# A two-block transformer kernel on one core: the shift of the modulation as products, squares on VectorE, work moved at three seams

## What is computed

```python
mod = (jnp.dot(jax.nn.silu(c), w_ada[l]) + b_ada[l])[:, None, :]
sh1, sc1, g1, sh2, sc2, g2 = jnp.split(mod, 6, axis=-1)
h = rmsnorm(x, norm_mix[l]) * (1.0 + sc1) + sh1
proj = jnp.dot(h, w_in[l])
...
x = x + g1 * jnp.dot(merged, w_out[l])
h2 = rmsnorm(x, norm_ffn[l]) * (1.0 + sc2) + sh2
y = hierarchical_moe(h2, ...)        # 4 groups x 8 experts, top 2 of a group
x = x + g2 * y
x = rmsnorm(x, norm_final)
...
h = rms_norm(x, norm1_g[l])          # second block: window attention and pooling
x = x + jnp.concatenate([a, b], axis=-1) @ w_out[l]
h2 = rms_norm(x, norm2_g[l])
x = x + peer(h2, ...)                # 16384 small experts, 8 heads x 16 of them per token
```

## Time and profile before

| | us |
|---|---|
| median of 3 runs | 2891.45 |
| lowest and highest | 2890.89, 2893.74 |
| the profiled execution's own time | 2890.11 |
| its span | 2888.3 |
| TensorE busy in it | 2725.0 (94%) |
| VectorE busy | 2064.0 (71%) |
| ScalarE busy | 1385.0 (48%) |
| GpSimd busy | 958.6 (33%) |

### The profile page before, as it was taken

One profiled execution on the slowest core, in us unless ns is written; L12 is line 12 of the kernel. 1 busy time (PEld: TensorE's weight loads), 2 busy tenths in 40 slices (PEclk: granted clock), 3 DMA queues, 4 the chain that ended last, 5 costly groups with the idle time before them and its releaser, 6 DMA issues. The chain is left out here.

```text
span 2888.3 us, 35914 instructions
## 1 busy us (share of the span) xinstructions
PE 2725.0 (94%) x13955; PEld 2395.2 (83%) x13955; DVE 2064.0 (71%) x2764; ACT 1385.0 (48%) x1865; POOL 958.6 (33%) x498
## 2 busy tenths in 40 slices
PE   5999998895999999999798899999999999999999
PEld 3778875684788888874676689999999999999999
DVE  7366645535898899970663589998888778888884
ACT  3232124422777777761342334368888633333332
POOL 2425441232222222220211347723333334444430
PEclk8999999996999999999889999999999999999999
DMA  6336321113899999975310325579999999999993
GB/s 264 102 122 243 117 88 44 54 51 140 315 370 382 389 373 359 361 299 242 137 44 1 117 85 171 183 266 343 347 349 353 358 350 372 380 364 375 371 351 110
DMA packets 173277, 703.45 MB, mean 244 GB/s; under 512 B 24720, under 2 KB 52016, under 8 KB 138800
## 3 DMA queue, kind: packets, MB, share of 16 engines
q1 hardware_dynamic: 89856, 459.49, 43.5%
q0 software_dynamic: 47232, 142.66, 13.3%
q10 hardware_dynamic: 36016, 98.97, 9.2%
HBM read 657.50 MB, written 72.88 MB: 253 GB/s over the span
## 5 line engine op out<-in xcount | busy, mean ns | idle before, releaser
L134 PE MATMUL psum<-h_high,pe_high 128*128 128x384 f32 (+1 forms) x1664 | 570.1, 343 | 15.3 <-DVE h_low L2412 9.4
L135 PE MATMUL psum<-h_low,pe_high 128*128 128x384 f32 (+1 forms) x1664 | 564.6, 339 | 0.0
L136 PE MATMUL psum<-h_high,pe_low 128*128 128x384 f32 (+1 forms) x1664 | 564.5, 339 | 0.0
L2148 ACT ACTIVATE pe_high<-ring 128x1024 fp32r<-128x1024 f32 x272 | 287.2, 1056 | 324.0 <-PE psum L136 323.6
L2275 DVE TENSOR_TENSOR pe_low<-ring,pe_high 128x1024 fp32r<-128x1024 f32 x216 | 264.5, 1225 | 191.3 <-ACT pe_high L2148 185.3
L128 POOL TENSOR_TENSOR mx_slab_low<-mx_half_slab,mx_slab_high 128x1024 fp32r<-128x1024 f32 x88 | 223.6, 2543 | 409.6 <-ACT mx_slab_high L119 395.5
L134 PEld LDWEIGHTS psum<-h_high,pe_high 128*128 128x128 f32 x1664 | 313.7, 188 | 21.5 <-issue 10.2
L1343 DVE TENSOR_TENSOR slab_low_moe<-half_slab_moe,slab_high_moe 128x2048 fp32r<-128x2048 f32 x126 | 285.6, 2289 | 50.2 <-ACT slab_high_moe L1292 50.1
L136 PEld LDWEIGHTS psum<-h_high,pe_low 128*128 128x128 f32 x1664 | 313.4, 188 | 5.2
L135 PEld LDWEIGHTS psum<-h_low,pe_high 128*128 128x128 f32 x1664 | 313.5, 188 | 4.6
L2033 POOL DMA_INDIRECT pe_rows<-in_v_rows,pe_place x128 | 204.0, 1594 | 258.5 <-DVE pe_sums L2382 222.0
(11 more groups left out here) (452 smaller groups left out, 5949.1 us busy)
## 6 DMA issues: line engine op xcount, KB each, us to landing
half_slab_moe<-in_weights SPq DMA_DIRECT2D x128, 1024.0 KB, 9.3
ring<-in_weights SPq DMA_DIRECT2D x162, 512.0 KB, 4.6
hT<-in_weights SPq DMA_DIRECT2D x64, 1024.0 KB, 7.4
ring<-in_v_rows SPq DMA_DIRECT2D x128, 512.0 KB
mx_half_slab<-in_weights SPq DMA_DIRECT2D x44, 1024.0 KB, 5.1
gates_rows<-pe_table ACTq DMA_DIRECT2D x12, 2048.0 KB, 10.5
pe_gt<-gates_rows ACTq DMA_DIRECT2D x16, 1536.0 KB
gelu_rows<-pe_gl ACTq DMA_DIRECT2D x30, 768.0 KB
```

Of the source, the lines that this page charges most:

```text
L134: pe.matmul(out, w[0], x[0], start=start, stop=False)
L135: pe.matmul(out, w[0], x[1], start=False, stop=False)
L136: return pe.matmul(out, w[1], x[0], start=False, stop=stop)
L2148: act.activation(high[:, g % RING, :], raw[:, g % RING, :], ACT.Copy).then_inc(highs, 1)
```

## The change

Four parts.

1. **Opening.** The shift half of the modulation becomes 16 fp32 products on TensorE: silu(c) spread over 128 columns (`c_wide`, 8 chunks) by the shift's weights (`w_shift`, 4 loads of 1 MB), two halves of 512; the wanted columns are taken out with the identity and a reduction on VectorE. They stand between the sums of squares and the distance products. The 8 scale columns remain dots; the root's reciprocal now stands ahead of them. The transfer of `c` as a row stands behind that of the constants.
2. **Mixer output.** The squares and their sum over chunks are made on VectorE behind each residual; four one-column products at the end give the sums per token.
3. **Route.** The wide root goes: the per-token root is spread over a diagonal (`spread_of`) and multiplied by ones, one fp32 product. The first slab's low part is on VectorE, in two halves (`first_low`), one ahead of the table's reading and one behind the names. Turns use two pairs of banks.
4. **Seams.** The waits for the experts' last landings go from the end of the experts to the end of overflow. The `share` matrices are made on VectorE at the start of overflow. The squares at the head of peer are made on VectorE in attend's output loop, with one product at that stage's end; ScalarE's root stands first in peer.

```diff
+            def scale_column(n):
+                if n >= 4:
+                    sp.wait_ge(dotted, n - 3)
+                c = 8 + n
+                sp.dma_start(ada[n % 4], d.w_ada[c // 4][:, (c % 4) * D:(c % 4 + 1) * D]).then_inc(ada_in[n % 4], 16)
...
+            for i in range(4):
+                sp.dma_start(w_shift[:, 2 * i:2 * i + 2, :], d.w_shift[:, 2 * i:2 * i + 2, :]).then_inc(w_shift_in[i], 16)
+            for n in range(4):
+                scale_column(n)
+            slab_half(0, 0)
+            for n in range(4, 8):
+                scale_column(n)
+            slab_half(0, 1)
...
+            pe.wait_ge(c_widened, 1)
+            for k in range(DC):
+                if k % 2 == 0:
+                    pe.wait_ge(w_shift_in[k // 2], 16)
+                for i in range(2):
+                    mm = pe.matmul(m.bank[i][:, :], c_wide[:, k, :], w_shift[:, k, i * 512:(i + 1) * 512],
+                                   start=(k == 0), stop=(k == DC - 1))
+            mm.then_inc(shift_mm, 1)
...
-                              start=(k == 0 and t == 0), stop=False)
-                pe.wait_ge(x_squared, k + 1)
-                for t in range(TT):
-                    pe.matmul(m.bank[4][:, 36 * TT + t:36 * TT + t + 1], x_squares[:, k % 2, t * P:(t + 1) * P], m.ones[:, 0:1],
-                              start=False, stop=(k == DC - 1 and t == TT - 1))
-                pe.matmul(m.bank[5][:, :], m.ones, x_squares[:, k % 2, :], start=(k == 0), stop=(k == DC - 1)
-                          ).then_inc(x_used, 1)
+                              start=(k == 0 and t == 0), stop=(k == DC - 1 and t == TT - 1))
...
+            pe.wait_ge(x_squared, 1)
+            for t in range(TT):
+                pe.matmul(m.bank[4][:, 36 * TT + t:36 * TT + t + 1], x_squares[:, 0, t * P:(t + 1) * P], m.ones[:, 0:1],
+                          start=True, stop=True)
...
+            act.dma_start(c_cols[:, :], d.c_cols).then_inc(cols_in, 16)
+            act.dma_start(m.const[:, :], d.const).then_inc(const_in, 16)
             act.dma_start(c_row, d.c.to_broadcast([P, D])).then_inc(c_in, 16)
...
+            act.wait_ge(cols_in, 16)
+            act.activation(c_wide, bcast(c_cols[:, :], 2, P), ACT.Silu).then_inc(c_widened, 1)
             act.wait_ge(x_in, 16)
             for k in range(DC):
                 act.activation(work[:, k, :], m.xT[:, k, :], ACT.Square).then_inc(squares_sem, 1)
+            act.wait_ge(c_in, 16)
+            act.activation(c_act, c_row, ACT.Silu).then_inc(c_ready, 1)
...
-            for i in range(8):
-                if i < 4:
-                    act_high(m, act, S_OUT + 1, i, 0)
-                act.wait_ge(mix_done, 9 + i)
-                if i >= 2:
-                    act.wait_ge(x_used, i - 1)
-                act.activation(x_squares[:, i % 2, :], m.xT[:, i, :], ACT.Square).then_inc(x_squared, 1)
+            for j in range(4):
+                act_high(m, act, S_OUT + 1, j, 0)
...
-            dve.wait_ge(c_ready, 1)
-            for t in range(6):
-                dots(t)
             dve.wait_ge(root, 1)
             chain(dve.reciprocal(rstd, rstd))
-            dots(6)
-            dots(7)
+            dve.wait_ge(c_ready, 1)
+            for n in range(4):
+                dot(n)
...
+            dve.wait_ge(shift_mm, 1)
+            own_columns = junk.rearrange("p (f n) -> p f n", n=P)
+            chain(dve.tensor_tensor(own_columns, m.psum[:, 0:2, :].rearrange("p b (f n) -> p (b f) n", n=P),
+                                    bcast(m.ident, 1, DC), ALU.mult))
+            chain(dve.tensor_reduce(m.raw[:, 0:8], own_columns, AX.X, ALU.add))
+            for n in range(4, 8):
+                dot(n)
...
+                chain(dve.scalar_tensor_tensor(out=m.xT[:, i, :], in0=m.bank[i % 4][:, :], scalar=m.mod[:, 16 + i:17 + i],
+                                               in1=m.xT[:, i, :], op0=ALU.mult, op1=ALU.add))
+                dve.sem_inc(mix_done, 1)
+                chain(dve.tensor_tensor(x_squares[:, min(i, 1), :], m.xT[:, i, :], m.xT[:, i, :], ALU.mult))
+                if i >= 1:
+                    chain(dve.tensor_tensor(x_squares[:, 0, :], x_squares[:, 0, :], x_squares[:, 1, :], ALU.add))
+            dve.sem_inc(x_squared, 1)
...
-            half = SLAB // 2
-            for h in range(2):
-                pool.wait_ge(m.highs, 4 * S_MOE + 2 * h + 2)
-                pool.tensor_tensor(m.low[:, 0, h * half:(h + 1) * half], m.half_slab[:, h, :],
-                                   m.high[:, 0, h * half:(h + 1) * half].bitcast(F32), ALU.subtract).then_inc(m.lows, 2)
...
-                if t >= 1:
-                    pe.wait_ge(rows_ready, 2 * t)
+                if t >= 2:
+                    pe.wait_ge(rows_ready, 2 * (t - 1))
                 for k in range(DC):
-                    mm = pe.transpose(m.bank[5 + k // 4][:, (k % 4) * P:(k % 4 + 1) * P], hT[:, k, t * P:(t + 1) * P],
+                    mm = pe.transpose(m.bank[2 * (t % 2) + k // 4][:, (k % 4) * P:(k % 4 + 1) * P], hT[:, k, t * P:(t + 1) * P],
...
+            pe.wait_ge(spread_ready, 1)
+            pe.matmul(m.bank[5][:, :], m.ones, flat(spread_of), start=True, stop=True).then_inc(spread, 1)
...
-            act.activation(rstd[:, :], m.bank[5][:, :], ACT.Sqrt, bias=m.eps[:, :], scale=1.0 / D).then_inc(root, 1)
...
+            def first_low(h):
+                dve.wait_ge(m.highs, 4 * S_MOE + 2 * h + 2)
+                dve.tensor_tensor(m.low[:, 0, h * half:(h + 1) * half], m.half_slab[:, h, :],
+                                  m.high[:, 0, h * half:(h + 1) * half].bitcast(F32), ALU.subtract).then_inc(m.lows, 2)
...
+            dve.tensor_tensor(spread_of[:, :, :], bcast(m.ident, 1, TT), bcast(col_std[:, :], 2, P), ALU.mult).then_inc(spread_ready, 1)
...
-            dve.wait_ge(root, 2)
-            chain(dve.reciprocal(rstd[:, :], rstd[:, :]))
+            dve.wait_ge(spread, 1)
             for k in range(DC):
                 dve.scalar_tensor_tensor(out=hT[:, k, :], in0=xT[:, k, :], scalar=scale[:, k:k + 1],
-                                         in1=rstd[:, :], op0=ALU.mult, op1=ALU.mult).then_inc(scaled, 1)
+                                         in1=m.bank[5][:, :], op0=ALU.mult, op1=ALU.mult).then_inc(scaled, 1)
...
+            first_low(0)
...
+            first_low(1)
...
-                pool.wait_ge(m.over_x_in[i], 16)
-                pool.wait_ge(y_out[i], 16 * E // 2)
...
-            pe.wait_ge(shares, 1)
...
+            pe.matmul(m.bank[5][:, :], m.ones, sq[:, 0, :], start=True, stop=True)
...
-                    last = dve.tensor_scalar(share[:, i, t, :], m.ident, m.pair_w[:, i, t:t + 1], None, ALU.mult)
-            last.then_inc(shares, 1)
...
+                chain(dve.tensor_tensor(m.xT[:, j, :], m.bank[j][:, :], m.xT[:, j, :], ALU.add))
+                chain(dve.tensor_tensor(sq[:, min(j, 1), :], m.xT[:, j, :], m.xT[:, j, :], ALU.mult))
+                if j >= 1:
+                    chain(dve.tensor_tensor(sq[:, 0, :], sq[:, 0, :], sq[:, 1, :], ALU.add))
+            dve.sem_inc(x_squared, 1)
...
-                pe.wait_ge(squares, norm * DC + k + 1)
-                mm = pe.matmul(m.bank[5][:, :], m.ones, work[:, k, :], start=(k == 0), stop=(k == DC - 1))
-            mm.then_inc(total, 1)
...
-                act.activation(work[:, k, :], xT[:, k, :], ACT.Square).then_inc(squares, 1)
+            act.activation(rstd[:, :], m.bank[5][:, :], ACT.Sqrt, bias=m.eps[:, :], scale=1.0 / D).then_inc(root, 1)
             split(0)
             split(1)
-            act.wait_ge(total, norm + 1)
-            act.activation(rstd[:, :], m.bank[5][:, :], ACT.Sqrt, bias=m.eps[:, :], scale=1.0 / D).then_inc(root, 1)
             split(2)
             split(3)
...
+            sp.wait_ge(m.over_gu[0], 32)
...
+                pool.wait_ge(m.over_x_in[i], 16)
+                pool.wait_ge(m.moe_y_out[i], 16 * EXPERTS // 2)
...
+            share = m.run[:, :, :].rearrange("p a (t n) -> p a t n", n=P)
+            for i in range(2):
+                dve.tensor_tensor(share[:, i, :, :], bcast(m.ident, 1, TT), bcast(m.pair_w[:, i, :], 2, P), ALU.mult)
```

75 lines of the change are left out of this document (32 added, 43 removed).

## The result

| | before | changed |
|---|---|---|
| median, us | 2891.43 | 2865.31 |
| lowest to highest (4 runs each) | 2890.89 to 2893.74 | 2863.64 to 2866.79 |
| span of the profiled execution | 2888.3 | 2865.0 |

The ratio is 0.9911, with an interval of 0.9899 to 0.9923: 26.1 us less, 0.9%. The prediction was 2867.9, with 2857 to 2877.

The account below looks back on a forecast made before the run. Long TensorE-bound stages with seams where TensorE waits for chains on other engines and landings; +4.0 - 12.7 - 12.4 - 3.0 - 0.9 + 1.5 = -23.5, from 2890.11 to 2866.6, plus 1.3 for the median: 2867.9, range 2857 to 2877.

Parts of the forecast that it names:

- Opening: Kernel start to first feature product: shift products on TensorE delay it, +4.0 us, ends -1.4 and +6.
- Mixer output: Mixer's output stage: shorter steps -10.6 us and a shorter tail -2.1, together -12.7, ends -14.7 and -10.8.
- Route: Route stage, starting at R (668.3 before): gather at R+29.7 instead of R+42.1, -12.4 us, ends -14 and -7.
- four of them 7.1, and the same 4.5: Route: four turns at pitch 1.77, then 4.5 us for table and names, would allow the gather at R+27.6.
- (a): Experts to overflow: GpSimd's waits for landings moved a stage later, -3.0 us, ends -3.3 and -1.5.
- (b): Overflow to attend: shares made earlier, the second row load's landing then latest, -0.9 us, range -1.5 to 0.
- (c): Attend to peer, whose stage starts at B: new head costs +1.5 us, ends -1.9 and +2.9.
- The tie: Peer head, starts 0.03 us apart: VectorE first, product at B+15.1 (+0.4); GpSimd first, B+17.6 (+2.9).
- VectorE first: Rival at the peer head: VectorE goes before GpSimd, net +0.4 instead of +1.5, total 2866.8; chance 0.12.
- the rule named beside it: Trainium skill, peer head: first issuer holds the shared pair all instruction, the other fully blocks; VectorE ahead gives +0.4.
- the opening was not hidden: Rival that opening costs 0 instead of +4.0 and route gets -14: -29.1, 2862.3 us; chance 0.18.
- no long stage ran at half clock: Slower-clock rival: experts' or peer's work at granted clock 0.50 cancels the gain or gives 2897; chance 0.04.

Follow-up runs that it names:

- run 4: The changed kernel with VectorE doing all 8 dots of the scale before it waits for the shift's products; 2863.6 us.
- Run 9: The kernel before with only the mixer output's squares and sum on VectorE, plus one more wide ones-product at its end; one execution 2880.9 us.
- run 2: The changed kernel with the peer head as before (8 squares on ScalarE, 8 products behind the barrier); 2863.4 us.
- run 3: The changed kernel with the peer head's wide root kept in PSUM, so a scaling has one SBUF input; 2861.2 us, 0.9893 of before.
- run 5: The changed kernel with the first expert slab's low part back on GpSimd, in front of the gather; one execution 2874.0 us.
- run 6: The changed kernel with the route's four turns on one pair of banks as before; one execution 2867.1 us.
- run 7: The changed kernel with GpSimd's waits for the last landings back at the experts' end, and that stage's own y tile; one execution 2868.2 us.
- run 8: The changed kernel with the 8 share instructions back at the start of the attend stage; one execution 2865.7 us.

## Why the prediction was right

**Opening, +4.0 said, +5.1 measured.** The step that failed is "the rounding of the first features comes near 44.9", behind the distance copies. The distance products took 5.42 at a granted clock of 0.97 to 1.00, where it had gone down to 0.50 midway in the kernel before and they took 7.3; so the copies ended at 41.7 and those roundings at 43.6. The path was VectorE's, for which the prediction had the first scaling at 43.4, and it came at 46.35. The sums started at 12.83 and took 9.28, so the shift's products ended 0.85 later than said; the dots had a pitch of 1.42 in place of 1.34, 0.3 for four; and the lock with GpSimd's low part (VectorE waiting for an instruction of GpSimd), which was put on the scaling of chunks, fell on `mod` (2.07 for 0.17). The 41.27 of the kernel before held such a lock already, the 43.4 held none. The +4.0 was taken with a part of a lock in it, so with the sign right, its size was under by 1.1 only. That VectorE's 2.8 us of idle time can be had by putting the shift's reading last is refuted (run 4).

**Mixer output, -12.7 said, -11.8 measured.** Steps of 6.35 were forecast and are 6.38, -10.4 for six of them; the tail gave 1.4, not 2.1. Run 9 shows the term alone.

**Route, -12.4 said, -15.9 measured**, beyond the -14 of its better end. The -12.4 counts to the gather, which came 14.3 sooner; 1.6 lie behind it. The last shift was forecast at R+16.0 and ended at R+15.0. The mis-sized steps lie behind it. The rows' landing was to hold the gather until R+29.7 and allowed R+27.8: the gather starts 3.7 after the last copy of turned rows at the earliest (runs 2 to 5). The other bound, "four of them 7.1, and the same 4.5", gave R+27.6, and R+27.7 came of it by another path, so its nearness is luck. The turns took 5.8, since the granted clock rose in the third of them, where all durations had been taken from rows at 0.50, but the table's products then waited for VectorE; and "the first low part on VectorE fits before the table" was wrong, as it held up the reading of the names by some 1.5. Both bounds end within 0.1 of each other in the changed kernel. The 1.6 behind the gather's start, which no row of before foretold, go with the later loads of the slabs. Runs 5 and 6 split the term: 12.3 hang on the low part's engine and 2.2 on the banks; the 1.4 left are for the root's row and its reciprocal, which no run has alone.

**Seams.** (a) -3.0 said and -3.0 measured at its place (run 7), of which 0.3 to 0.4 is paid back at the end of overflow: the landings are long done there, as was said, but the waits for them were put at nothing. (b) -0.9 said, -1.1 measured from the attend stage's start (run 8). (c) +1.5 said, +2.3 measured. The tie went to GpSimd: by the recorded starts VectorE's first scaling was 0.01 ahead, the condition of the rival "VectorE first", but it waited from its start (2.91), while GpSimd's low part ran at its own speed (2.35). So a row that is 0.01 ahead doesn't tell who comes first, and neither the rival's price nor the rule named beside it was put to the test. Of the two cases the bad one came, and it was 0.9 too dear: the first product came at B+16.7 in place of B+17.6. The stage itself started 2.7 later, as said (2.6). Runs 2 and 3 show the seam from both sides.

**The sum.** -23.5 said; the six terms measured -24.4 (with -1.1 for the shares), and 1.1 is the net of what came in stretches without an edit and of the waits paid back in overflow. So the total agrees closer than its terms do, and that is luck: opening, output and peer head were 2.8 too favourable, the route 3.5 too unfavourable. The 2.6 us between 2867.9 and the median come of the step from the profiled execution to the median: 1.3 was added for it, and in the changed kernel the median lay 1.5 below (2865.3, and 2866.8 for the profiled execution, where 2866.6 was forecast). Of the other rivals none came: the opening was not hidden, the experts didn't wait for transfers, and no long stage ran at half clock, though the short falls are that rival in small: 1.7 us each.

## What to carry to other kernels

A stage between two long ones is worth what its chain is: price each seam from the last product before it to the first behind it, and look there for small instructions that take several us (here 4.55 for 16 elements of a partition) before anything else; moving the work that blocked them gave more in this stage (12.3 of 15.9) than the rest of its edits. It also put a low part into VectorE's own path, so look where the moved work lands. Where VectorE and GpSimd both read SBUF, one operand in PSUM is enough to free VectorE (0.69 in place of up to 2.91 for a scaling); with queues on both sides they took turns here, so each VectorE instruction waited once. Moving 8 columns' dots to TensorE as fp32 products, with the order of transfers that went with it, cost 5.1 us more than it saved, and VectorE waited for them; each part of such a change is worth timing alone.
